# The fourth convolution tile on GpSimd, two memory steps on other engines, and a new list that orders the recurrence's heads

## What is computed

```python
def second_block(x, mem, ...):
    mem_n = rms_norm(mem, mem_norm_g)
    h = rms_norm(x, g[0])
    p = h @ w_in_first
    y_conv = conformer_conv(p[..., :2 * D_CONV], ...)      # D_CONV = 512
    y_rwkv, v_first = rwkv7_mix(p[..., 2 * D_CONV:], ...)  # 8 heads of 64
    y = jnp.concatenate([y_conv, y_rwkv], axis=-1) @ w_out[i]
    x = x + rms_norm(y, g[1])
    y = memory_cross_attention(rms_norm(x, g[2]), mem_n, wq[i], wkv[i], wo[i])
...
def conformer_conv(u, conv_w, conv_b, ln_g, ln_b):
    h = u[..., :D_CONV] * jax.nn.sigmoid(u[..., D_CONV:])
    h = lax.conv_general_dilated(                          # depthwise, CONV_WIDTH = 31 taps, causal
        h, conv_w[:, None, :], window_strides=(1,), padding=[(CONV_WIDTH - 1, 0)],
        dimension_numbers=("NWC", "WIO", "NWC"), feature_group_count=D_CONV) + conv_b
    h = layer_norm(h, ln_g, ln_b)
    return jax.nn.silu(h)
...
def rwkv7_recurrence(r, w, k, v, kk, a):
    def step(S, inp):
        s_kk = jnp.einsum("bhvk,bhk->bhv", S, kk_t)
        S = (S * w_t[:, :, None, :] - s_kk[..., None] * (kk_t * a_t)[:, :, None, :]
             + v_t[..., None] * k_t[:, :, None, :])
        return S, jnp.einsum("bhvk,bhk->bhv", S, r_t)
...
def memory_cross_attention(h, mem_n, wq, wkv, wo):
    kv = mem_n @ wkv
    km = kv[..., :D_MODEL].reshape(B, M, XA_HEADS, XA_HEAD_DIM)
    vm = kv[..., D_MODEL:].reshape(B, M, XA_HEADS, XA_HEAD_DIM)
```

## Time and profile before

| | us |
|---|---|
| median of three executions | 1607.04 |
| the profiled execution | 1607.06 |
| its span from first to last instruction | 1605.2 |
| PE busy in the span | 1562.3 |
| DVE, ACT, POOL busy | 820.0, 609.6, 380.0 |

### The profile page before, as it was taken

The page is one execution under the profiler, slowest core; times in us unless marked ns, Lnnn a source line. Parts: engine busy times, 40 slices in busy tenths (PEclk is TensorE's granted clock), DMA queues, the critical chain, the costliest instruction groups (busy, mean ns, idle before and its releaser), DMA issues. The chain is left out here.

```text
span 1605.2 us, 26943 instructions
## 1 busy us (share of the span) xinstructions
PE 1562.3 (97%) x11520; PEld 1285.4 (80%) x11520; DVE 820.0 (51%) x1262; ACT 609.6 (38%) x977; POOL 380.0 (24%) x319
## 2 busy tenths in 40 slices
PE   8999999999999999999999899999999999999997
PEld 7897778888888888888877777779779888888877
DVE  6886523653333333355687977547527432333334
ACT  5444423344232231443465654434345322222222
POOL 0121211212011010241174341022023420330234
PEclk9999999999999999999999999999999999999999
DMA  6243122242323223233222111123122233232211
GB/s 244 80 139 121 59 76 79 92 144 79 105 79 106 82 102 105 79 105 123 100 81 80 36 40 65 55 106 106 53 79 72 86 105 105 79 104 85 100 62 70
DMA packets 30998, 147.27 MB, mean 92 GB/s; under 512 B 3232, under 2 KB 8992, under 8 KB 15904
## 3 DMA queue, kind: packets, MB, share of 16 engines
q1 hardware_dynamic: 30880, 145.56, 26.2%
HBM read 139.26 MB, written 6.29 MB: 91 GB/s over the span
## 5 line engine op out<-in xcount | busy, mean ns | idle before, releaser
L169 PE MATMUL ps<-zr,wh 128*128 128x512 f32 (+2 forms) x4028 | 1164.8, 376 | 9.6 <-ACT wh L178 6.9
L169 PEld LDWEIGHTS ps<-zr,wh 128*128 128x128 f32 x4028 | 724.2, 190 | 158.5 <-ACT wh L178 7.2
L169 PE MATMUL ps<-zr,wl 128*128 128x512 f32 (+2 forms) x2008 | 743.1, 372 | 0.0
L181 POOL TENSOR_TENSOR zf<-zf 128x512 f32<-128x512 f32 (+1 forms) x230 | 272.6, 1192 | 713.7 <-ACT zf L175 482.8
L169 PEld LDWEIGHTS ps<-zr,wl 128*128 128x128 f32 x2008 | 378.2, 189 | 71.3
L181 DVE TENSOR_TENSOR wl<-raw,wh 128x1024 fp32r<-128x1024 f32 (+2 forms) x243 | 302.6, 1285 | 197.9 <-ACT wh L178 197.6
L178 ACT ACTIVATE wh<-raw 128x1024 fp32r<-128x1024 f32 (+2 forms) x243 | 240.5, 1037 | 176.1 <-PE ps L169 173.7
L175 ACT ACTIVATE zf<-zf 128x512 f32<-128x512 f32 (+2 forms) x232 | 127.8, 561 | 366.5 <-DVE zf L181 251.9
L181 DVE TENSOR_TENSOR zf<-ps,zf 128x512 f32<-128x512 f32 (+3 forms) x172 | 98.2, 578 | 169.4 <-PE ps L169 142.9
L169 PE MATMUL ps<-zf 64*64 64x64 f32 (+6 forms) x3800 | 155.2, 243 | 14.3 <-issue 4.1
L169 PEld LDWEIGHTS ps<-zf 64*64 64x64 f32 (+3 forms) x3800 | 117.6, 145 | 51.9 <-issue 34.1
(11 more groups left out here) (91 smaller groups left out, 581.4 us busy)
## 6 DMA issues: line engine op xcount, KB each, us to landing
raw<-in_wstream SPq DMA_DIRECT2D x116, 1024.0 KB, 4.8
zf<-in_xT SPq DMA_DIRECT2D x16, 256.0 KB, 3.1
raw<-in_wstream SPq DMA_DIRECT2D x4, 768.0 KB, 4.1
x_scratch<-zf SPq DMA_DIRECT2D x8, 256.0 KB, 2.1
zf<-x_scratch SPq DMA_DIRECT2D x8, 256.0 KB, 4.9
out<-zf SPq DMA_DIRECT2D x16, 128.0 KB, 1.7
zf<-in_cu SPq DMA_DIRECT2D x1, 1256.0 KB, 8.9
zf<-in_memT SPq DMA_DIRECT2D x1, 1024.0 KB, 5.7
```

The source lines that it names most:

```text
L169: return self.raw.matmul(out_, l, x, start=start, stop=stop)
L181: return self.raw.tensor_tensor(out_, a, b, o)
```

## The change

Three pieces of work change their engine, and the list changes.

- Tile 3 of the convolution is wholly `tap.g`, and with the bias in its first tap. `CSH`, `LAST`, `CP` and `conv.join` are gone. DVE loses five taps and the joining addition; ACT gains five scaled copies and POOL five additions, and POOL's first tap is now the form with two scalars, as for tile 0.
- `ev.vm` is an ACT copy with a scale per row in place of a DVE instruction, with the same waits, the one for the earlier store among them.
- `mem.x2` is one step for two tiles. ACT makes both high parts, then scales both sources where they lie (two more copies); POOL subtracts the high part of both tiles in one 128 x 512 instruction. DVE has no part in it.
- Buffers: slot 58 is now tile 3 of the convolution, and slot 23 the sum for its normalisation and an output tile of `wa`.
- `TURNS` is a new list. It has six letters `c` fewer (81 to 75) and five `g` more (58 to 63); the counts of the others and of the dots are the same. Steps outside the list stand as they did.

```diff
-CSH = 26
-LAST = {1: 30, 2: 30, 3: 30 - CSH}
...
 TURNS = """
-...ppp.p...p.p..pppp..g..cgcc.pcgc.pgpgp.c.cggggcc.cpch.ccchhghgcggg.ccghcgch.cghg.ghh.ghgch.pcggghc
+.......p.p.p.pggg.gp..g.g.pp.ggppcggcc..gp.p.gcpppc.cphc.gccgghghc..hchgggcgcc.hccgccc.cp.hpchghgpch
...
-        yield from taps(3, 31 - CSH, 31, "g")
+        yield from taps(3, 0, 31, "g")
...
-        for i in range(1, 4):
+        for i in range(1, 3):
...
-        put("conv.join")
-        yield
...
         for k in range(0, 8, 2):
-            put("mem.x2", k)
-            put("mem.x2", k + 1)
+            put("mem.x2", k // 2)
...
+            def ev_vm(n, mt):
+                uu = n - pl.base["vm"][0]
+                e.wait_ge(("mm", "t.vm", n, mt), ("mem.rs.rt",), ("kv.out", 3 + uu, mt) if uu else None)
+                e.cp(vm_out[mt], ps("t.vm", n, mt)[:, 0:256], scale=tn_of("mem.rs")[:, mt:mt + 1]).then_inc(*e.up("t.vm", n, mt))
+
+            def mem_x2(j):
+                e.wait_ge(("mem.in2", j), *[(("mm", "head.rt", 0, 0), ("mm", "head.rt", 0, 1)),
+                                            (("t.p", 13),), (("p.w", 12),), (("p.w", 13),)][j])
+                for k in (2 * j, 2 * j + 1):
+                    e.cp(mem2_hl(k)[0], mem2_src(k), scale=vec("mem_norm_g_2", k)).then_inc(*e.up("mem.h2", k))
+                for k in (2 * j, 2 * j + 1):
+                    e.wait_ge(("mem.h2", k))
+                    e.cp(mem2_src(k), mem2_src(k), scale=vec("mem_norm_g_2", k)).then_inc(*e.up("mem.g2", k))
...
-            def mem_x2(k):
-                lo_scaled(("mem.x2", k), mem2_hl(k)[1], mem2_src(k), vec("mem_norm_g_2", k), mem2_hl(k)[0], "mem.h2", k)
...
-                e.ts(vm_out[mt], ps("t.vm", n, mt)[:, 0:256], tn_of("mem.rs")[:, mt:mt + 1],
-                     MUL).then_inc(*e.up("t.vm", n, mt))
...
+            def mem_x2(j):
+                h, l = [28, 68, 42, 43][j], [56, 57, 47, 48][j]
+                e.wait_ge(("mem.g2", 2 * j + 1))
+                e.tt(R(l), F(l), rb(R(h)), SUB).then_inc(*e.up("mem.x2", j))
```

55 lines of the change are left out of this document (21 added, 34 removed).

## The result

The changed kernel takes 1608.77 us (median of 20 executions, 1603.57 to 1616.40), the kernel before 1604.59 us (20 executions beside them, 1602.25 to 1608.69). The ratio is **1.0026, 95% interval 1.0017 to 1.0036**. The forecast was 1600.8 us from 1607.06, a change of -6.3 us; the measured one is +4.2 us. So the forecast was wrong in its sign and by 10.5 us. By the prediction's own bound of 0.3% the change makes no difference, and what there is of one is a loss.

What follows compares the result with a forecast made beforehand. DVE's queue was taken to pace PE from 878 to 940 us, with round trips counting as much after it. 1607.06 - 5.8 - 2.5 - 1.4 + 1.5 + 1.2 + 0.7 = 1600.8 us; range 1593 to 1611.5 us.

Steps and rivals of the forecast that it cites:

- (a): 878 to 940 us: DVE paces PE, so the 5.8 us taken off DVE there count in full.
- (b): 940 to 1012 us: DVE is busy 71%, so 40% of 6.3 us off DVE is won, 2.5 us.
- (c): 878 to 1012 us: a quarter of PE's 5.4 us of lost clock comes back, 1.4 us.
- (d): 760 to 878 us: earlier taps delay head steps on which PE waits; cost 1.5 us, bounds 0 and 5.3.
- (e): At the end: three more bare state steps, each 0.39 us of idle PE; cost 1.2 us.
- (f): Nine more POOL instructions reading SBUF lengthen DVE's by 0.149 us each; PE feels half, cost 0.7 us.
- Rival 4: Each of nine new POOL instructions blocks a DVE instruction for its whole 1.3 us; 1609.4 us, chance 0.04.
- rival 3: From tile 3's first tap to the last `vm` tile, ACT's queue takes DVE's place; 1612.8 us, chance 0.14.
- ACT's cover: ACT's idle third covers its 10.7 us of added work, costed at nothing on PE's path.
- Rival 2: Round trips between PE and DVE take the relief's place; 1607.3 us, covering 1603 to 1611, chance 0.17.
- The sign for (a): 878 to 1012 us: PE idle 8 to 11 us, not 16.4; wrong if DVE idles more and PE as now.

Runs made afterwards that it cites:

- old_relief: Kernel before, old order: memory subtractions, tile 3's five taps and join cut to 8 columns on DVE, values' evacuation on ACT; 0.9997 of the kernel before.
- old_all_relief: `old_relief` with nearly all the convolution's taps also cut to 8 columns on DVE, ACT and POOL; 1602.36 us, 0.9977 of the kernel before.
- new_relief: The same relief as `old_relief`, in the new list's order; 1.0045 of the kernel before.
- the first experiments: Runs parting work from order, against the kernel before: old work in new list 1.0091; changed kernel with memory's low parts back on DVE 1.0059, values' evacuation back 1.0040.
- old_newtail: All the changed kernel's work, old order up to the convolution's last output and new order from there; 1.0053 of the kernel before.
- old_moves_noscale: All three moves in the old order, with ACT's eight in-place scalings of the memory tokens left out; 1.0014 of the kernel before.
- old_vm: Kernel before in its own order with only the memory values' evacuation moved to ACT; 1.0000 of the kernel before.

## Why the prediction was wrong, step by step

- **What bounds the kernel.** "DVE's queue sets the pace of PE" up to 940 us is the step that failed. It was read from DVE's 91% beside PE's idle 10.2 us and from the names in PE's waits. `old_relief` (0.9997) and `old_all_relief` (0.9977, with DVE at 62%) show that PE idles there all the same; that it is in its own round trips is the most likely reading, and not measured by itself. The sign I had at hand and didn't weigh: DVE waited for PE too, 14.5 us in 24 waits.
- **(a) and (b), -8.3 us.** In the old order they are worth 0, by `old_relief` -0.5 (+-2.4, for a relief that they would have priced at about 6 us), and the three moves with their costs +3.2 us. In the new order they are worth 10 us against the old work there (7 by `new_relief` on an equal list), and most of it as clock. The price that the order asks decides them, and I priced them in the old order, without asking what the new one puts next to them.
- **(c), -1.4 us.** Of all executions the share of clock lost, one less the mean granted clock, times the span, is 13.4 us after and 14.4 before (mean of 20 executions, and of the 17 beside the first experiments). The difference of 1.0 us is uncertain by 2, so (c) is neither confirmed nor refuted, and the clock is not where the gain went. The place that (c) names does not bear it out: the profiled clock from 878 to 1012 us is 0.95 after and was 0.96. The clock goes with much of the scatter: within the changed kernel the executions at 0.990 or less of the clock took 1610.3 to 1616.4 us.
- **(d), +1.5 us.** By the runs about 2 us, with an interval that holds zero; by the trace 1.8 us of waiting and at least 1.7 us of clock, of which a part is caught up later. The wait stands where the step had it, behind the bunched taps. PE's waits for DVE from 760 to 878 us are 2.7 + 0.7 = 3.4 us, where they were 1.8, which passes the 3 us that the prediction had set as the sign of being wrong in (d).
- **(e), +1.2 us.** Measured 4.3 us. The row of a bare step (0.39 us) was right, but not the number of them: three stand in the timeline where there were two, one more and not three. The term is larger all the same. `fin.yc` ahead of them is bare too and costs 1.04 us, and the clock falls there in three of seven profiles (1.7 us in `old_newtail`'s). The rest of the 4.3 us is not accounted for.
- **(f), +0.7 us.** Measured 2.1, not told apart from 0.7 by the runs; but DVE's held-up instructions cost it 5.4 us more, where the step had 1.3, though in profiles with POOL's old work they cost up to 3.3 us more as well. The mean of a row (0.838 against 0.689 us) hid that single instructions wait out a whole POOL instruction. I gave the mechanism 0.04 and argued against it with that mean. The Trainium skill, page SBUF — State Buffer, section Who interferes with whom, says that the second of the two is blocked until the first has ended. Here the trace agrees to the full length (1.28 us for 0.17), and the taps, with one input in SBUF and one in PSUM, stay out of it (749 ns), as the page has it. What the page's rule doesn't give is how often they meet: 15 times here, where it was 8, and 11 and 12 with POOL's old work. Rival 4's change of +2.3 us and rival 3's of +5.7 lie on both sides of the measured one, but by accident: both take the relief as real and lose it again, and in the old order no run shows that the change's relief was ever worth anything.
- **ACT's cover held.** The two kernels on ACT's part (`old_moves_noscale`, `old_vm`) move by 1 us or less (uncertain by 2 to 3), and ACT's waits for POOL fell to 2.1 us, far from the 15 at which rival 3 was to decide. Rival 3 did not happen.
- **Rival 2** gave 1607.3 us from 1607.1, that is no change, with the round trips in the relief's place. It was the right case for the old order, and had 0.17. Of the new order's own gain and loss it says nothing.
- **The sign for (a)** came true in half: DVE idles 32.7 us from 878 to 1012 us in place of 26.6, and PE 13.6 in place of 16.4, where 8 to 11 were forecast.

In sum: moved work +3.2, start +2, middle -4.5, end +4.3 make +5.0 us, against +4.2 measured; each of the four is uncertain by 2 to 3 us.
